# Attention kept by channels from the gate to the out projection, softmax scaled before its transposes, and looser edges between the stages of a two-layer kernel

## The reference, cut to what matters

```python
h = _rmsnorm(x, g_pre) * (1.0 + scale) + shift
aq, ak, av, ag, rkv, rg, gq, gkk, gv, gg = split(h @ w_in)
attn = sliding_window_attention(aq, ak, av, sinks) * silu(ag)     # 8 query heads, 2 key heads of 64
rwkv = rwkv7_mixer(...) * silu(rg)                                # 4 heads of 64; kk = k * k_k, normalized per head
gla  = gla_mixer(...) * silu(gg)                                  # gated linear attention, 4 heads
y = concatenate([attn, rwkv, gla]) @ w_out
x1 = x + gate * _rmsnorm(y, g_post)
```

## Time and profile before

| | us |
|---|---|
| median of 3 runs (3609.08 to 3612.58) | 3611.74 |
| the profiled execution, its own time | 3611.44 |
| its span | 3609.7 |
| TensorE busy | 3497.7 (97%) |
| VectorE busy | 1910.8 (53%) |
| ScalarE busy | 1585.6 (44%) |
| GpSimd busy | 417.0 (12%) |

### The profile page before, as it was taken

The page is one execution under the profiler, slowest core; times in us unless marked ns, Lnnn a source line. Parts: engine busy times, 40 slices in busy tenths (PEclk is TensorE's granted clock), DMA queues, the critical chain, the costliest instruction groups (busy, mean ns, idle before and its releaser), DMA issues. The chain is left out here.

```text
span 3609.7 us, 69211 instructions
## 1 busy us (share of the span) xinstructions
PE 3497.7 (97%) x28060; PEld 2660.5 (74%) x28060; DVE 1910.8 (53%) x4800; ACT 1585.6 (44%) x3591; POOL 417.0 (12%) x689
## 2 busy tenths in 40 slices
PE   6999999997999999989999999999999999999998
PEld 5887788766666666578778887777886677777765
DVE  5223333247777777534788788666683343333322
ACT  2223233323444444313677666777753344443320
POOL 0000000005444444310000000000000000000000
PEclk9999999998999999999999999999999999999999
DMA  9111111123222222241111114121215212111121
GB/s 314 54 54 48 54 54 54 54 86 147 84 77 81 76 76 76 90 132 48 50 54 62 53 52 168 56 66 60 69 46 194 74 53 78 42 49 67 48 84 41
DMA packets 134963, 282.05 MB, mean 78 GB/s; under 512 B 26640, under 2 KB 86048, under 8 KB 127136
## 3 DMA queue, kind: packets, MB, share of 16 engines
q1 hardware_dynamic: 125968, 267.75, 21.0%
q0 software_dynamic: 2304, 8.39, 0.6%
q10 hardware_dynamic: 6416, 2.08, 0.2%
HBM read 181.72 MB, written 96.47 MB: 77 GB/s over the span
## 5 line engine op out<-in xcount | busy, mean ns | idle before, releaser
L2575 ACT ACTIVATE at_pT<-at_bank 128x512 f32<-128x512 f32 (+3 forms) x320 | 154.4, 531 | 535.1 <-PE at_bank L2474 534.8
L1976 PEld LDWEIGHTS p_bank<-p_hT,w_in_rest 128*128 128x128 f32 x3072 | 345.5, 192 | 14.5 <-issue 12.4
L1976 PE MATMUL p_bank<-p_hT,w_in_rest 128*128 128x128 f32 x3072 | 350.2, 276 | 1.6 <-DVE p_st L2256 1.3
L2097 ACT ACTIVATE p_r<-p_acc,p_mid 128x384 f32<-128x384 f32 (+13 forms) x224 | 292.9, 1308 | 58.8 <-DVE p_acc L2283 54.4
L306 PE MATMUL p_bank<-p_hT,w_in_rest 128*128 128x128 f32 x2080 | 267.3, 275 | 0.0
L1115 PE MATMUL b_banks<-b_wout,b_yT 128*128 128x512 f32 x512 | 248.0, 610 | 3.7 <-DVE b_yT L1457 2.2
L306 PEld LDWEIGHTS p_bank<-p_hT,w_in_rest 128*128 128x128 f32 x2080 | 249.9, 192 | 0.0
L2515 PE MATMUL at_bank<-arena,at_y 128*128 128x512 f32 x512 | 239.8, 599 | 4.1 <-DVE at_y L2625 2.5
L1967 PE MATMUL p_bank<-arena,p_hT 128*128 128x512 f32 (+2 forms) x768 | 241.9, 467 | 1.3 <-ACT p_hT L2091 1.3
L2155 ACT ACTIVATE p_r<-p_bank,ahead_rows 128x512 f32<-128x512 f32 (+3 forms) x304 | 167.9, 635 | 156.5 <-PE p_bank L2070 144.5
L2058 PE MATMUL p_bank<-p_hTg,arena 128*128 128x256 f32 x1024 | 226.7, 381 | 1.7 <-ACT arena L2119 1.7
(11 more groups left out here) (419 smaller groups left out, 6240.6 us busy)
## 6 DMA issues: line engine op xcount, KB each, us to landing
stage<-p_st SPq DMA_DIRECT2D x15, 1856.0 KB, 5.9
arena<-stage SPq DMA_DIRECT2D x15, 1856.0 KB, 7.5
at_rest<-stage SPq DMA_DIRECT2D x16, 1280.0 KB, 5.9
stage<-p_pr SPq DMA_DIRECT2D x128, 128.0 KB, 1.8
p_ada<-in_ada_w SPq DMA_DIRECT2D x8, 1024.0 KB, 9.2
p_xt<-in_x SPq DMA_DIRECT2D x16, 512.0 KB, 3.2
b_x<-in_x SPq DMA_DIRECT2D x16, 512.0 KB, 3.2
x<-b_x SPq DMA_DIRECT2D x16, 512.0 KB, 3.1
```

Of the source, the lines that this page charges most:

```text
L1976: last = mm(bank[:, m * P:(m + 1) * P], weights(k, c + m * P, c + (m + 1) * P), hTs[:, n % 2, k, :], start=(k == 0), stop=(k == KD - 1))
L2097: ch.link(f(flat(r[:, :, :])[:, 0:L], acc[:, slot.buf_a, 0:L], ACT.Sign, scale=-1.0, bias=m, accum_out=tally[:, 0:1]))
```

## The change

1. *The gate by channels.* In the first projections `ag` is projected with `channels`, its weight columns reordered so that a block of 128 holds head i of both key heads. `stage1` then holds the gate in the layout of `attend`'s result.
2. *Attention stays by channels.* ScalarE copies attend's bank straight to y, POOL multiplies there, and `dense` uses y itself for its first four chunks. `turn_attended`, `attended`, `turn_y(., 0)`, the copy of that half to yT and their banks go. Rows of w_out are loaded in the same order. Only piece 2 of `dense` waits for yT.
3. *The division comes first.* ScalarE takes all exponentials in two groups of four heads, VectorE the reciprocals, and ScalarE then scales the probabilities by them before they are transposed.
4. *Orders.* On TensorE `Z(a, 2)` stands ahead of `dense(o, 3)`, and `state_products(b, 1)` between the second and third `turn_probs`. On VectorE `maxima` stands ahead of `out_sum`, and `denominators` ahead of `join_X(a, 1)`.
5. *Tile 0's keys.* kk and kn of tile 0 are made in the last tile of the first projections, on VectorE and POOL. The mixers' masks are loaded first, under a semaphore of their own.
6. *Edges.* The buffers x and pr are one buffer outside both stages; the waits for x1's stores and for the gate stores move to where their data is overwritten or read.

The diff, cut to its core:

```diff
@@ first_projections
+                at = place(C_AG)
+                for k in range(KD):
+                    for g in range(A_KV):
+                        sp.dma_start(w_in(k, at, at + 512).rearrange("p (c g d) -> p g c d", g=2, d=HEAD)[:, g],
+                                     wsrc[:, k, C_AG + 256 * g:C_AG + 256 * g + 256].rearrange("p (c d) -> p c d", d=HEAD)).then_inc(S["ag_weights"], 16)
-                fetch_weights("ag", (C_AG, C_RKV))
...
+                pool.wait_ge(S["tile_early"], 32)
+                ch.link(nc.gpsimd.tensor_scalar(less, ahead["rows"][:, 1, :], -1.0, 1.0, ALU.mult, ALU.add))
+                ch.link(pool_tt(kn, wa_1, ahead["rows"][:, 1, :], ALU.mult))
+                pool.wait_ge(S["kk_summed"], 1)
+                pool_tt(lengths[:, 4:8], lengths[:, 0:4], spread(numbers[:, 0:1], [P, 4]), ALU.pow).then_inc(S["kk_length"], 1)
+                ch.link(pool_tt(kn, kn, less, ALU.add))
+                pool_tt(kn, kn, k_1, ALU.mult).then_inc(S["kn_made"], 1)
...
-                    tokens(B[7][:, :], C_AG, 512).then_inc(S["ag_proj"], 1)
+                    for c in range(4):
+                        last = channels(B[7][:, c * P:(c + 1) * P], C_AG, c * P)
+                    last.then_inc(S["ag_proj"], 1)
...
+                    if not tile.more:
+                        dve.wait_ge(S["tile_early"], 32)
+                        ch.link(tt(kk, k_1, ahead["rows"][:, 0, :], ALU.mult))
+                        ch.link(tt(kk_squares, kk, kk, ALU.mult))
+                        ch.link(v.tensor_reduce(lengths[:, 0:4], heads(kk_squares), AX.X, ALU.add))
+                        ts(lengths[:, 0:4], lengths[:, 0:4], 1e-24, None, ALU.max).then_inc(S["kk_summed"], 1)
+                        dve.wait_ge(S["kk_length"], 1)
+                        tt(heads(kk), heads(kk), spread(lengths[:, 4:8].unsqueeze(2), [P, 4, HEAD]), ALU.mult).then_inc(S["kk_made"], 1)
                     dve.wait_ge(S["act_staged"], n)
@@ mixers, PE
     def dense(n, piece):
         if piece == 0:
-            for e in range(2):
-                pe.wait_ge(S[f"yt{e}_taken"], n + 1)
+            pe.wait_ge(S["att_gated"], n + 1)
...
+        if piece == 2:
+            pe.wait_ge(S["yt1_taken"], n + 1)
         for k in range(2 * (piece % 4), 2 * (piece % 4) + 2):
-            last = mm(OUT[:, :], yT[:, k, :], wout[:, k, half * 512:(half + 1) * 512], start=(k == 0), stop=(k == KD - 1))
+            part = ys[:, n % 3, k * P:(k + 1) * P] if k < 4 else yT[:, k - 4, :]
+            last = mm(OUT[:, :], part, wout[:, k, half * 512:(half + 1) * 512], start=(k == 0), stop=(k == KD - 1))
...
-                        turn_y(o, 1)
-                        turn_y(o, 0)
+                        turn_y(o)
...
                         XY_products(a, 1)
+                    if valid(a):
+                        Z(a, 2)
                     if valid(o):
                         dense(o, 3)
                     if valid(a):
                         turn_probs(a, 0)
-                        Z(a, 2)
                         turn_probs(a, 1)
+                    if valid(b):
+                        state_products(b, 1)
+                    if valid(a):
                         turn_probs(a, 2)
                         turn_probs(a, 3)
-                    if valid(b):
-                        state_products(b, 1)
...
-                        turn_attended(a)
@@ mixers, ACT
+                def exponentials(n, g):
+                    act.wait_ge(S["max_ready"], n + 1)
+                    first = 0 if n else P
+                    for h in range(4 * g, 4 * g + 4):
+                        f(s[:, h, first:], s[:, h, first:], ACT.Exp, bias=nm[:, h:h + 1], accum_out=den[:, h:h + 1])
+                    if g == 1:
+                        f(am[:, :], am[:, :], ACT.Exp).then_inc(S["sink_exp"], 1)
+
                 def probabilities(n, j):
...
+                    if j == 0:
+                        act.wait_ge(S["den_ready"], n + 1)
                     for e in range(2):
                         h = 4 * (j % 2) + 2 * (j // 2) + e
-                        last = f(s[:, h, first:], s[:, h, first:], ACT.Exp, bias=nm[:, h:h + 1], accum_out=den[:, h:h + 1])
+                        last = f(s[:, h, first:], s[:, h, first:], ACT.Copy, scale=den[:, h:h + 1])
...
-                    f(flat(s[:, 0:2, :]), bank_of("attT", n), ACT.Copy).then_inc(S["attT_taken"], 1)
+                    f(ys[:, n % 3, 0:512], bank_of("attT", n), ACT.Copy).then_inc(S["attT_taken"], 1)
...
-                        turned_y(o)
                         first_X(a)
+                        exponentials(a, 0)
                         take_Z(a, 1)
-                        probabilities(a, 2)
+                        exponentials(a, 1)
                         probabilities(a, 0)
                         probabilities(a, 1)
-                        probabilities(a, 3)
                     if valid(o):
                         out_squares(o, 0)
...
+                        probabilities(a, 2)
                         take_Z(a, 2)
+                        probabilities(a, 3)
                         turned_probs(a, 0)
@@ mixers, DVE
                         biased(a, 1)
+                        maxima(a)
                     if valid(o - 1):
                         out_sum(o - 1)
                     if valid(a):
-                        maxima(a)
                         gla_near(a)
+                        denominators(a)
                         join_X(a, 1)
...
-                        denominators(a)
...
-                        attended(a)
@@ edges
-                sp.wait_ge(S["x1_stored"], 16 * TILES)
...
-                for b in range(2):
-                    sp.wait_ge(S[f"gates_stored{b}"], 32 * PAIRS * GATE_CHUNKS // 4)
...
+                        if ORDER[n + 1] == TILES - 2:
+                            for b in range(2):
+                                sp.wait_ge(gates_stored[b], 32 * PAIRS * GATE_CHUNKS // 4)
```

More of the change, by code:

```diff
@@ L168, in first_projections @@
         w_head = arena[:, 0:W_HEAD * (IN1 + GK1)].rearrange("p (k n) -> p k n", n=IN1 + GK1)
+        wa_1, k_1 = arena[:, M_WA + R_W:M_GQ], arena[:, M_RKV + R_W:M_RKV + 2 * R_W]
+        kk, kn, less = (arena[:, 2 * M_END + e * R_W:2 * M_END + (e + 1) * R_W] for e in range(3))
+        kk_squares, lengths = arena[:, 2 * M_END + 3 * R_W:2 * M_END + 4 * R_W], arena[:, 2 * M_END + 4 * R_W:2 * M_END + 4 * R_W + 8]
+        heads = lambda ap: ap.rearrange("p (h d) -> p h d", d=HEAD)
         moved = {C_AV: C_AG + 384, C_AG: C_AV}
@@ L301, in _, with channels @@
                     i, n, hT = tile.t, tile.n, hTs[:, tile.b]
-                    def channels(out, c):
+                    def channels(out, c, more=0):
+                        at = place(c) + more
                         for k in range(KD):
-                            last = mm(out, w_in(k, place(c), place(c) + P), hT[:, k, 1:P + 1], start=(k == 0), stop=(k == KD - 1))
+                            last = mm(out, w_in(k, at, at + P), hT[:, k, 1:P + 1], start=(k == 0), stop=(k == KD - 1))
                         return last
@@ L609, with mixers @@
 HEAD2 = KD * 1064
-def mixers(nc, A, stage1, x1, arena, arena_loaded, x_early, keep, const, ahead):
+def mixers(nc, A, stage1, x1, arena, arena_loaded, x_early, keep, const, ahead, x, x1_stored):
     ident = const["ident"]
@@ L729, in _ @@
                 wsrc = A["w_out"][0].rearrange("(k p) n -> p k n", p=P)
-                for k in range(0, KD, 2):
+                for g in range(A_KV):
+                    sp.dma_start(wout[half_of(g), 0:4, :], A["w_out"][0][256 * g:256 * g + 256, :].rearrange("(c d) n -> d c n", d=HEAD)).then_inc(S["wout_loaded"], 16)
+                for k in range(KD // 2, KD, 2):
                     sp.dma_start(wout[:, k:k + 2, :], wsrc[:, k:k + 2, :]).then_inc(S["wout_loaded"], 16)
@@ L1066, in attend @@
                     last.then_inc(S["attT_done"], 1)
-                def turn_attended(n):
-                    pe.wait_ge(S["attT_taken"], n + 1)
-                    bank = bank_for("att", n)
-                    for i in range(4):
-                        last = tr(bank[:, i * P:(i + 1) * P], flat(s[:, 0:2, :])[:, i * P:(i + 1) * P], ident[:, :])
-                    last.then_inc(S["att_done"], 1)
                 def gla_round(n, turn):
@@ L1760, with projections @@
 N_WEIGHTS = 16 * 6
-def projections(nc, A, x1, arena, head_loaded, x_early, rest, stage, hTd, chosen, KT, VC, tables, early, const, spare_rows, first_at):
+def projections(nc, A, x1, arena, head_loaded, x_early, rest, stage, hTd, chosen, KT, VC, tables, early, const, spare_rows, first_at, pr, x1_stored, gates_stored):
     ident = const["ident"]
@@ L2368, in blocks_before, with attention @@
     return sum(len(blocks(ORDER[k // PAIRS_A])) for k in range(step))
-def attention(nc, A, x1, stage, chosen, out, KT, VC, wo, const, first_at):
+def attention(nc, A, x1, stage, chosen, out, KT, VC, wo, const, first_at, gates_stored):
```

(8 more changed lines are left out.)

100 lines of the change are left out of this document (47 added, 53 removed).

## The result

The changed kernel takes **3625.26 us** (median of 7 runs, 3620.55 to 3629.13) against 3611.74 us (7 runs beside it, 3608.41 to 3613.59): a ratio of 1.0036, 95% interval 1.0027 to 1.0045. It is slower by 13.5 us. The forecast was 3614.0 us, no change that can be told, with a range of 3602 to 3624 us; the time is 1.3 us above the range, on the side of rival 2.

A forecast was written before the change was run, and what follows sets the result against it. TensorE was taken to bound projections and mixers, with no wait left in a 43.58 us period. Terms 4.5 - 3.4 + 0.4 + 6.6 + 1.0 - 2.0 - 2.8 - 1.7 = +2.6 us gave 3614.0 us, range 3602 to 3624.

The forecast's parts named there:

- rival 2: Mixers: softmax chain becomes the bound, denominators waiting for ScalarE's last exponential ahead of the join; 3623 us, chance 0.19.
- Gate, 4.5 + 0.4: First projections: gate by channels costs 0.28 us in 16 tiles, +4.5; VectorE's new block for tile 0's keys, +0.4.
- Rival 3: First tile: gate's weights come late in small pieces, +2 us, 3616; shares 0.57 with the forecast and another rival.
- Edge to the mixers, -3.4: Mixers' start: tile 0's key work gone from POOL, so ScalarE copies the first turned vectors sooner, -3.4 us.
- Stall A, 0.8: Mixers' period: TensorE waits for VectorE's join before the inverse's second level; 0.7 to 1.1 us, 0.8 taken, floor 0.6.
- Stall B, 0.65: Mixers' period: TensorE waits for ScalarE's scaled probabilities before the fourth transpose; 0.3 to 1.0 us, 0.65 taken.
- The period's net, +0.47: Mixers' period: two new waits, 0.8 and 0.65, less 0.98 for eight dropped transposes; +0.47 us, x 14 = +6.6.
- Opening periods, +1: Mixers' two opening periods: same two waits, no squares and half the gain; +1 us, between 0 and 2.
- Drain and edges, -2, -2.8, -1.7: Mixers' last rounds -2 us; edge into second projections -2.8; edge into attention -1.7, stores no longer waited for there.
- The frame of the sum: Terms summed to +2.6 us on a profiled execution of 3611.44, 0.3 below the median 3611.74, giving 3614.0.

The follow-up runs named there:

- the repeat: The changed kernel run and profiled once more with no edit: median 3625.05 us, ratio 1.0038.
- the run with ScalarE's order mended: Changed kernel with ScalarE scaling probabilities 2 and 3 ahead of the out projection's squares, TensorE's new order kept: 3608.81 us, ratio 0.9996.
- the experiment with the denominators: Changed kernel with VectorE's denominators placed behind join_X of the first level instead of ahead: 3620.93 us, ratio 1.0031.
- the run with both edits: Changed kernel with the inverse's second level back behind dense(o, 3) and probabilities 2 and 3 scaled ahead of the squares: 3603.48 us, ratio 0.9981.
- the mended order and the waits at the stage ends: Changed kernel, TensorE's reorderings undone, probabilities 2 and 3 ahead of the squares, both stage-end waits put back: 3605.62 us, ratio 0.9985.

## Why the prediction was wrong, by its steps

**Gate, 4.5 + 0.4: right.** The block takes 7.14 us in the first tile of the trace (81.99 to 89.13, where the earlier trace rows has 6.87), and the start moved by 4.8. The gate alone gave 4.1, so the rest, with the new block for tile 0's keys, is 0.7 where 0.4 stood. Rival 3 did not happen. SP's queue:

```profile
66.83 5.41 SPq L222 DMA_DIRECT2D arena<-in_w_in  x6
72.27 5.50 SPq L222 DMA_DIRECT2D w_in_rest<-in_w_in  x10
```

All 16 transfers are issued by 77.8, sooner than the 81 of the prediction: each took 0.68 us of SP's queue, not the 0.95 of the query weights. TensorE wants them from 81.99, 4.2 us later, and doesn't wait. The Trainium skill speaks against pieces under 512 B (DMA: Bandwidth & Descriptors, Specifications); in this trace they cost no time.

**Edge to the mixers, -3.4: right in size, then given back.** ScalarE copies the first turned vectors 8.96 us after the mixers' first load (822.02 - 813.06), where it was 12.08 in the earlier trace rows: 3.1 us sooner. At the third tile's load 2.0 us were left, in the repeat 0.6; the granted clock of this stretch was 0.86 and 0.75, and 0.74 before.

**Stall A, 0.8: right.** The wait was 0.73 in the period shown (and it alone is the 0.73 of the run with ScalarE's order mended), between 0.55 and 1.13 in single periods. The step's working from the floor of 0.6 is what the experiments found: order 0.59, denominators 0.14. POOL's contention came in part: in the period shown the add took 0.34, and it is the rest of the running POOL instruction that counts, as the experiment with the denominators shows. The reciprocal isn't like the add, as the step had it: it took 0.20 with POOL at work and without. By the rule of the Trainium skill (GPSIMD Engine Reference, Specifications) alone A would have been 1.1 every time; in 13 periods it was 1.03 and 1.13 once each.

**Stall B, 0.65: nearly right.** The chain of the step is there: 2.80 us from the end of the piece to the last turn (1225.53 to 1228.33), where it had 2.8, over 2.1 of cover. By the period, B is 44.32 - 42.77 - 0.73 = 0.82 us. Only half of that is shown as waiting, 0.41; 0.12 is a gap before the third turn that the view doesn't mark (1227.15 to 1227.27), and 0.30 stand in the busy time: with ScalarE's order mended the same matmuls in the same order show 42.77 us.

**The period's net, +0.47: this step failed**, with the right mechanism and two terms mis-sized, stall B and the transposes. It was +0.77 (0.64 in the repeat). By the rows, B is 0.82 us where 0.65 was forecast (A and B together 1.55, not 1.45), and the eight transposes are 0.81 where 0.98 was taken off. The price of one from a run of twelve, 0.12, was too high for one that is dropped: 0.10. Together 0.3 us a period; the 14 rounds and the drain are 4.1 us above the forecast.

**Opening periods, +1: this step failed too.** One round alone, the second tile's, grew by 3.0 us. TensorE in it:

```profile
868.89 0.68 PE L1019 MATMUL b_banks<-b_Z,b_XY 64*64 64x64 f32 x16 [1.61 <-ACT b_Z L1238]
871.96 1.12 PE L1009 MATMUL b_banks<-b_XY,b_cT 64*64 64x64 f32 x16 [1.92 <-DVE b_XY L1454]
```
```profile
871.01 0.37 DVE L1537 TENSOR_TENSOR b_den<-b_den,b_am 128x8 f32<-128x8 f32 x1 [0.98 <-ACT b_am L1278]
```
```profile
860.89:902.46 41.57, 32.24 (x541) 25.36 (x534) 30.77 (x83) 19.66 (x69) 19.88 (x28) 0.92 0.16 58
```

Before, the same round waited once in this place, 1.81 us for VectorE's masked copies of the gla's products (L1495). With no out projection in it, TensorE comes for Z while ScalarE is still in the first four exponentials, which now stand ahead of taking it and had to wait for the maxima: 1.61 us. Then it waits 1.92 us for the join: VectorE's denominators stand ahead of that and wait 0.98 us for ScalarE's last exponential, until 871.01. That is the mechanism of rival 2, in this one round. The granted clock falls to the lower level behind the two waits (0.92 over the round, 0.96 before). The prediction had listed these exponentials under rival 2, in the steady period, and didn't look at the round where they have no cover. That the second level's order doesn't do this is shown: with that order undone the round still takes 41.1 to 41.5 us (42.6 in the run with both edits), and with it alone on the kernel before 38.9. That the new softmax does is read from the rows; no run has it alone. With the denominators behind the join the second wait is 0.59 us, but the clock is then lower (0.88) and the round takes 41.1. No experiment was aimed at mending it.

**Drain and edges, -2, -2.8, -1.7: near enough.** From the last tile's load to the last store, two full periods and the drain, the mixers are 0.7 us shorter; with 0.77 for each period the drain gave 2.3. The edges gave 2.2 and 1.5. TensorE now starts 1.95 us behind the issue of the last store, not 1.4.

**The frame of the sum.** It was made against one execution and carried over to the median. That held before (0.3 us apart) and not after (4.7). The two traces differ by 9.1 us; the forecast for this was 2.6, and the missing 6.5 are the periods (4.1), the opening (0.9 and 2.5), the edges (0.8), and against them a shorter attention stage (1.7; its start had a clock of 0.91 where it was 0.87). Why the changed kernel's executions are more often at 0.991 and below (8 of 12, where 11 of 70 of the kernel before were, in the sets run beside the experiments) stays open. The two stalls of the period aren't needed for it: with both edits 6 of 11 were, and with the mended order and the waits at the stage ends 7 of 11. That the extra waits in the opening bring the clock down is seen in one round only.

**Rivals.** The time landed beside rival 2's 3623, for the most part by another way. In the steady periods ScalarE's last exponential ended about 0.33 us before the denominators' add began, so they never bound there; they did in the second tile's round. Stall A rose by 0.14 us from them, and the probabilities 2 and 3 waited for the squares, not for the denominators. That the time came so near the range, and the forecast's sum to within 6.5 us in the traces, owes something to luck: the attention stage gave back 1.7 us that no term of the sum had.

## What to carry to other kernels

A piece of work moved ahead of a filler loses the filler's cover and takes its own away from whatever is behind the filler; count both. In an in-order queue look for the instruction that waits (here the squares) with ready work behind it: putting two scaled copies ahead of it was worth nearly as much (16 us) as putting TensorE's order back (18 us). Cost the rounds without fillers one by one, and compare a stall's price by whole periods, since the view of waits can show half of it.

## What the runs showed of the hardware

- A wait need not show as idle time. In the changed kernel 0.30 us a period of waiting for ScalarE are inside TensorE's busy time, whose ends are modelled: 43.07 us for 584 matmuls that show 42.77 in the same order when ScalarE isn't late. The view gave 0.41 us in 0.82.
- A VectorE add of two SBUF inputs with 8 columns (0.17 us alone) that starts while a POOL instruction runs ends with that instruction: at 1311.35 where POOL's product ended at 1311.32, having taken 0.64 us. Over the steady periods of all 14 traces 184 of 189 such adds took 0.17 us or ended within 0.03 us of POOL's running instruction; in four of the other five both started within 0.02 us and the add went first.
- The 14 profiled executions, of 12 kernels, spent 38 to 75 us each at the lower TensorE clock, nearly all of it around the start of a stage: in the first 50 us, between 800 and 890, 1530 and 1580, 2710 and 2750, and in the last 60. The time of the changed kernel was 5.2 us apart between executions of clock 0.992 and above and those below.
